# Two more block products of the first layer's MLP up-projection by seven products in place of eight

## What is computed

```python
h2 = rmsnorm(x, g_mlp)                                   # 256 x 1024
x = x + jnp.square(jax.nn.relu(h2 @ w_up)) @ w_down      # w_up 1024 x 4096, w_down 4096 x 1024
```

## Time and profile before

| | us |
|---|---|
| median of 3 runs | 979.6 |
| lowest and highest | 979.2, 980.6 |
| the profiled execution | 979.45 |
| its span in the trace | 977.6 |
| TensorE busy in the span | 969.5 |
| VectorE busy | 759.6 |
| ScalarE busy | 518.2 |

### The profile page before, as it was taken

How to read it: one execution, slowest core, us unless ns; L and a number is a source line. 1 busy time by engine, 2 the same in 40 slices (tenths; PEclk the granted TensorE clock), 3 DMA queues, 4 the chain that set the end, 5 groups by cost and what they waited for, 6 DMA issues and landing times.

```text
span 977.6 us, 12897 instructions
## 1 busy us (share of the span) xinstructions
PE 969.5 (99%) x5174; PEld 811.5 (83%) x5174; DVE 759.6 (78%) x848; ACT 518.2 (53%) x619; POOL 129.2 (13%) x101
## 2 busy tenths in 40 slices
PE   9999999999999999999999999999999999999997
PEld 7888888888888888888888888888887899799696
DVE  5878886766978766778886776988777788789984
ACT  6656553465566445556563464543487454644352
POOL 0000000000000000000000010000000159269820
PEclk9999999999999999999999999999999999999999
DMA  9887796669972994697796669899774957346351
GB/s 361 305 281 277 237 270 211 232 222 321 344 234 86 268 270 129 186 302 250 249 272 209 225 226 245 260 281 287 239 248 140 295 179 259 131 164 160 107 194 44
DMA packets 142684, 224.78 MB, mean 230 GB/s; under 512 B 11808, under 2 KB 50720, under 8 KB 142368
## 3 DMA queue, kind: packets, MB, share of 16 engines
q1 hardware_dynamic: 142624, 223.95, 72.0%
HBM read 199.32 MB, written 22.28 MB: 227 GB/s over the span
## 4 chain that ended last, share of the span: by engine, by line
PE 98%; DMA 1%; DVE 0%; ACT 0%; issue 0%; POOL 0%; DVEq 0%; SPq 0%; ACTq 0%
PE bank L1061 15%; PE bank L1064 15%; PE bank L1063 15%; PE bank L1084 13%; PE bank L1088 12%; PE bank L1095 12%; PE bank L1507 2%; PE bank L1808 1%; PE bank L1616 1%; PE bank L1579 1%; PE bank L1199 1%; PE bank L1176 1%; PE bank L1289 1%; PE bank L1795 1%; PE bank L1093 1%; PE bank L1086 1%
## 5 line engine op out<-in xcount | busy, mean ns | idle before, releaser
L2348 DVE TENSOR_TENSOR w_lo<-arena,w_hi 128x2048 fp32r<-128x2048 f32 (+1 forms) x84 | 192.6, 2301 | 52.3 <-ACT w_hi L1903 51.9
L2348 DVE TENSOR_TENSOR w_lo<-raw,w_hi 128x2048 fp32r<-128x2048 f32 (+1 forms) x76 | 173.6, 2290 | 56.9 <-ACT w_hi L1903 56.7
L1903 ACT ACTIVATE w_hi<-arena 128x2048 fp32r<-128x2048 f32 (+1 forms) x84 | 158.7, 1891 | 82.1 <-PE bank L1064 71.5
L1903 ACT ACTIVATE w_hi<-raw 128x2048 fp32r<-128x2048 f32 (+1 forms) x81 | 153.1, 1891 | 73.8 <-PE bank L1064 61.2
L1061 PE MATMUL bank<-w_hi,hT 128*128 128x512 f32 (+1 forms) x336 | 129.5, 385 | 0.0
L1064 PE MATMUL bank<-w_hi,hT 128*128 128x512 f32 (+1 forms) x320 | 122.8, 384 | 0.0
L1063 PE MATMUL bank<-w_lo,hT 128*128 128x512 f32 (+1 forms) x320 | 122.8, 384 | 0.0
L1084 PE MATMUL bank<-w_hi,hT 128*128 128x512 f32 (+1 forms) x316 | 121.5, 386 | 0.0
L1088 PE MATMUL bank<-w_hi,hT 128*128 128x512 f32 (+1 forms) x316 | 120.9, 384 | 0.0
L3230 POOL TENSOR_TENSOR rstd<-mean,const 128x1 f32<-128x1 f32 (+1 forms) x16 | 9.1, 576 | 615.9 <-DVE mean L2357 456.7
L1095 PE MATMUL bank<-w_lo,hT 128*128 128x512 f32 (+1 forms) x316 | 82.8, 384 | 0.0
(11 more groups left out here) (375 smaller groups left out, 1799.1 us busy)
## 6 DMA issues: line engine op xcount, KB each, us to landing
arena<-in_w_in SPq DMA_DIRECT2D x21, 1024.0 KB, 6.4
raw<-in_w_in SPq DMA_DIRECT2D x20, 1024.0 KB, 6.8
arena<-in_w_down SPq DMA_DIRECT2D x20, 1024.0 KB, 6.4
raw<-in_w_up SPq DMA_DIRECT2D x18, 1024.0 KB, 7.5
arena<-in_w_up SPq DMA_DIRECT2D x14, 1024.0 KB, 7.8
raw<-in_w_down SPq DMA_DIRECT2D x12, 1024.0 KB, 7.2
arena<-u_bounce SPq DMA_DIRECT2D x72, 128.0 KB, 4.7
u_bounce<-arena SPq DMA_DIRECT2D x17, 512.0 KB, 6.3
```

The lines of the kernel that those rows point to most:

```text
L1903: act.activation(w_hi[:, p % SPLIT_RING, :, 0:n], raw_at(p)[:, :, 0:n], copy).then_inc(hi_ready, 1)
L2348: dve.tensor_tensor(w_lo[:, s, :, 0:n], raw_at(p)[:, :, 0:n], w_hi[:, s, :, 0:n].bitcast(F32), ALU.subtract).then_inc(lo_ready, 1)
```

## The change

`PAIRED` becomes `(4, 6)`: groups 4 and 5 are a pair too. The steps are up 0, 1, 2, down 0, up 3, first 4, down 1, rest 4, down 2, down 3, first 6, rest 6, down 4 to 7. So the first pair's five products stand right behind up 3, and the seven products of the second pair stand in a row. The sums of the token operands are made once and serve both pairs; the weight differences are made for each pair. The four raw pieces of the second pair go into slots that the first pair has used up (six slots for both pairs, `PAIR_B11` and so on). The product that went to bank 7 in `pair_rest` goes to bank 6. For the second pair ScalarE waits, before it copies the first product, until the store of group 5 has landed (`rows_stored`), and TensorE waits for the banks of both groups of the first pair. In SP's order the four loads of groups 4 and 5 stand earlier, and those of groups 6 and 7 behind waits for the sums "first 0" and "second 0" and for splits of the first pair.

```diff
-PAIRED_STEPS = [("up", 0), ("up", 1), ("up", 2), ("down", 0), ("up", 3), ("down", 1), ("up", 4), ("up", 5), ("first", 6),
-                ("down", 2), ("rest", 6)] + [("down", f) for f in range(3, F_GROUPS)]
-SUMS_AFTER = {1: ("rows 2",), 3: ("rows 0",), 4: ("rows 1", "third"), 5: ("rows 3",), 6: ("first", "second"), 9: ("fourth",)}
+PAIRED_STEPS = [("up", 0), ("up", 1), ("up", 2), ("down", 0), ("up", 3), ("first", 4), ("down", 1), ("rest", 4), ("down", 2),
+                ("down", 3), ("first", 6), ("rest", 6)] + [("down", f) for f in range(4, F_GROUPS)]
+SUMS_AFTER = {1: ("rows 2", "rows 0"), 2: ("rows 1",), 3: ("rows 3", "third 0"), 4: ("first 0", "second 0"), 6: ("fourth 0",),
+              8: ("third 1",), 9: ("first 1", "second 1"), 10: ("fourth 1",)}
...
-PAIRED = (6,)
+PAIRED = (4, 6)
...
-PAIR_B11, PAIR_B12, PAIR_B22, PAIR_B21, PAIR_T3, PAIR_T2 = ((i,) for i in range(6))
+PAIR_B11, PAIR_B12, PAIR_B22, PAIR_B21 = (0, 1), (1, 0), (2, 4), (3, 2)
+PAIR_T3, PAIR_T2 = (4, 5), (5, 3)
...
-TURNED_IN = [{2: 0, 3: 1, 5: 2, 7: 3, 11: 4, 12: 5, 13: 6, 14: 7}, INNER_TURNS]
+TURNED_IN = [{2: 0, 3: 1, 6: 2, 8: 3, 10: 4, 12: 5, 13: 6, 14: 7}, INNER_TURNS]
...
                 up(2, 0)
+                load_pair(0, PAIR_B12, 1, 1)
                 up(2, 1)
+                load_pair(0, PAIR_B22, 1, 0)
                 down(0, 0)
                 down(0, 1)
                 store_up(l, 0)
+                load_pair(0, PAIR_B11, 0, 1)
                 up(3, 0)
                 fetch_up(l, 0)
-                load_pair(0, PAIR_B12, 1, 1)
                 up(3, 1)
+                load_pair(0, PAIR_B21, 0, 0)
                 store_up(l, 1)
...
                 for t in range(T):
-                    pe.wait_ge(out_free[t], n - 1)
+                    pe.wait_ge(out_free[t], n if i else n - 1)
...
-                pe.wait_ge(pair_sum, 3 * i + 2)
-                pair_product(p, 7, *pair_sums(3), False).then_inc(piece_used, 1)
+                pe.wait_ge(pair_sum, 3 * i + 1)
+                pair_product(p, 6, *pair_sums(3), True).then_inc(piece_used, 1)
...
                         act.wait_ge(piece_used, q + 1)
+                        if f != PAIRED[0]:
+                            act.wait_ge(rows_stored, 16 * (2 * T + f + 1))
                         act.activation(pair_p1, bank[:, 0, :], copy).then_inc(pair_taken, 1)
...
                     if kind == "first":
                         step(q + 2)
+                        if i == 10:
+                            operand_sum("fourth 1")
                         step(q + 3)
                         pair_base(PAIRED.index(f))
                         step(q + 4)
```

More of the change, by code:

```diff
@@ L106 @@
         PAIR_PIECES[at] = PAIR_SLOT + slots[i]
-PAIR_SUMS = {FIRST_OF[0] + 1: "third", FIRST_OF[0] + 4: "first", FIRST_OF[0] + 3: "second", REST_OF[0] + 1: "fourth"}
+PAIR_SUMS = {}
+for i in range(len(PAIRED)):
+    PAIR_SUMS.update({FIRST_OF[i] + 1: f"third {i}", FIRST_OF[i] + 4: f"first {i}", FIRST_OF[i] + 3: f"second {i}",
+                      REST_OF[i] + 1: f"fourth {i}"})
 ANGLES_AT = 2
@@ L2627, in operand_sum @@
                 elif name == "rows 1":
-                    for i, a in enumerate(hidden(1, 0)):
-                        order.link(dve.tensor_tensor(full[1], full[i], a, ALU.subtract))
+                    for src, a in enumerate(hidden(1, 0)):
+                        order.link(dve.tensor_tensor(full[1], full[src], a, ALU.subtract))
                     parts(1)
@@ L2635, in operand_sum @@
                     parts(3)
-                elif name == "third":
-                    dve.wait_ge(middle_landed, 16 + 32)
+                elif kind == "third":
+                    dve.wait_ge(middle_landed, 16 + 32 * (i + 1))
                     weights(PAIR_T3, PAIR_B22, PAIR_B12)
-                elif name == "first":
-                    dve.wait_ge(pair_outer, 32)
+                elif kind == "first":
+                    dve.wait_ge(pair_outer, 32 * (i + 1))
                     weights(PAIR_B12, PAIR_B12, PAIR_B11)
-                elif name == "second":
+                elif kind == "second":
                     weights(PAIR_T2, PAIR_B22, PAIR_B12)
                 else:
-                    piece_split(dve, FIRST_OF[0] + 2)
+                    piece_split(dve, FIRST_OF[i] + 2)
                     weights(PAIR_B21, PAIR_B21, PAIR_T2)
@@ L2680, in pair_second @@
                 order.settle()
-                order.link(dve.tensor_tensor(by_block(pair_c), by_column(bank[:, 7, :]), by_column(pair_w), ALU.add))
+                order.link(dve.tensor_tensor(by_block(pair_c), by_column(bank[:, 6, :]), by_column(pair_wp), ALU.add))
                 square_rows(pair_wp, pair_c).then_inc(out_free[0], 2)
@@ L2897, in _ @@
                         for name in SUMS_AFTER.get(i, ()):
-                            if name != "fourth":
+                            if not name.startswith("fourth"):
                                 operand_sum(name)
```

37 lines of the change are left out of this document (21 added, 16 removed).

## The result

| | before | after |
|---|---|---|
| median | 979.4 us (4 runs) | 998.3 us (4 runs, 997.5 to 999.8) |
| profiled execution | 979.45 | 999.78 |
| its span | 977.6 | 997.9 |
| TensorE busy | 969.5 | 973.8 |
| VectorE busy | 759.6 | 780.0 |

The changed kernel is slower: ratio 1.0193, with an interval of 1.0175 to 1.021. That is 18.9 us by the medians and 20.3 us from one profiled execution to the other. The forecast was 992.9, the range 985.0 to 999.0.

The account below looks back on a forecast made before the run. The prediction took TensorE to bound the kernel, with no slack, so each wait costs one for one. It summed -2.7 + 4.2 + 1.0 + 7.0 + 3.8 = +13.3 us to 992.9 us, range 985.0 to 999.0.

Parts of the forecast that it names:

- the second rival with its lower bounds: Rival: only VectorE delays, the queue's loads go through in idle time; 986.9 us, chance 0.22; lower bounds set the range's 985.0.
- Place 1: First two fetches: 3 MB more loads ahead of each delay down 0 and the first pair; +4.2 us.
- Place 2: Last product of rest 4: a transposition and uT_lo ahead of `pair_fourth` use up the conversion's slack; +1.0 us.
- Place 3: Second pair, seven products in a row: the seventh waits for VectorE's list of splits, differences and steps; +7.0 us.
- Place 4: Down 6: its rows, from the seventh product, come late after VectorE's steps, store and fetch; +3.8 us.
- 28.7 against 21.8: Second pair, us from the first down 3 piece's end: VectorE's list against TensorE reaching the seventh product; 6.9 late.
- 2 us of it I give back: Before down 6: store and fetch taken 2 us under the earlier 16.7, group 5's fetch no longer being queued.
- R + 9.7: Before down 6: VectorE's steps take 9.7 us from R, the start of the second pair's seventh product.
- R + 24.5: TensorE wants down 6 24.5 us after R, the seventh product's start: that product plus down 4 and 5.
- Nothing gives it back: Whole sum of +13.3 us: TensorE runs on at the same pace behind each wait.
- the clock falls as well: Rival: TensorE's clock halves behind three waits, some 1.5 us each, +4.5 in all; 997.4 us, chance 0.13.
- All is hidden: Rival: no waits, only the 2.7 us saved; 976.9 us, needing VectorE's second-pair list 7 us shorter; chance 0.05.

Follow-up runs that it names:

- the kernel with six waits: Kernel before the change, with six waits put in front of down 1 to down 6 of the second layer's MLP: 1014.8 us (one execution).
- The kernel with the new order: Changed kernel with both SP queue edits and VectorE's pair steps and some differences placed earlier, no work taken from VectorE: 979.1 us, ratio 0.9999.
- short differences and the new order: New-order kernel with three more VectorE moves, and the second pair's four weight differences formed over 16 of 512 columns: 977.0 us, ratio 0.9978.
- the kernel kept busy: Changed kernel with unread matmuls on TensorE in its waits: 12 before rest 6, 11 within it, 24 before down 6: 996.0 us, ratio 1.0165.
- short differences: Changed kernel with the second pair's three weight differences formed over 16 of 512 columns only: 996.3 us, ratio 1.017.
- the loads for down 6 first: Changed kernel with the two loads for down 6 ahead of the stores of groups 6 and 7 in SP's queue: 991.1 us, ratio 1.0108.

## Why the prediction was right, and where it was not

The direction was right, and so was the reason for it: each of the four places lost time. The size was short, +13.3 for +18.9, and 998.3 lies only 0.7 us inside the range; the profiled execution is outside it. The upper end of 999.0 had room for bigger terms or for the clock, not for both, and that it still held the result is in part luck. (Its lower end, "the second rival with its lower bounds", sums to 984.4 and not 985.0.)

| term | forecast | measured in the profiled execution |
|---|---|---|
| 12 matmuls saved | -2.7 | -2.7 |
| 1. first two fetches | +4.2 | 3.3, with small pauses 3.5 |
| 2. last product of rest 4 | +1.0 | 1.5, with the pauses behind it 2.0 |
| 3. second pair in a row | +7.0 | 0.9 + 3.1 + 2.9 = 6.9, with small pauses 7.1 |
| 4. down 6 | +3.8 | 6.1 |
| lower clock | 0 (rival: +4.5) | +4.4 |
| sum | +13.3 | +20.4 (20.3 between the executions) |

- **What bounds the kernel**: right. Every wait put in front of TensorE was lost one for one; the kernel with six waits shows the same where nothing else changes.
- **Place 1**: the mechanism is shown by its undoing (3.5 us back), and the size was 0.7 too high. The second transposition was 3.8 late, not 4.7.
- **Place 2**: the mechanism agrees with the view of waits, TensorE waits for `w_hi` of the difference "fourth" there; no run priced it alone. Mis-sized by 1.0. The prediction sets 2.4 us of new work against 2.3 of slack, which gives about 0; it took 1.0. In the changed kernel VectorE also came to `pair_base` 1.3 us later beside TensorE (274.89, where down 1 begins at 273.50; before, 302.35 and 302.28), and behind the conversion TensorE had pauses of 0.5 in sum for its split.
- **Place 3**: the sum (28.7 against 21.8) met the wait within 0.1, and the three waits came where they were said to come. But the reading that a shorter list would shorten the wait was wrong by half: with 6.7 us of differences taken away only 3 us of waits went. Beside the list stands the order: two splits between `pair_base` and `pair_fourth`, the second of which needs the slot of the fifth product. The kernel with the new order has the same work for VectorE (busy 779.9 us, 780.0 in the changed kernel) and none of these three waits; one of 1.0 for a split is left there. And cured at this place alone, the time comes back at down 6.
- **Place 4**: the step that failed is "2 us of it I give back". Store and fetch took 16.2 us (348.6 to 364.8), as long as the 16.7 of the earlier trace rows, since 2 MB for down 6 are issued between the store and the fetch in both kernels. Before, the wait for them was hidden. Without that rebate the prediction's own sum is 6.5, not 4.5, and it then took 3.8 for it; 6.1 was measured. Two more differences nearly cancel: VectorE's part was 1.8 longer (R + 11.5 for R + 9.7; the rows give 10.3 for the steps that it names, and 1.2 are idle time for a conversion that waits for the seventh product), and TensorE came 1.7 later than R + 24.5, for the clock.
- **"Nothing gives it back: behind each wait TensorE runs on at the same pace"**: wrong. The forecast gave 0.13 to the case that the clock falls as well, and priced it at 4.5 us; it came true at 4.4, beside all four terms. That the sizes agree is in part luck: it named three falls of 1.5 us, and there were two, of 9 and 13 matmuls. The sentence of the Trainium skill (TensorE: Matmul & The Clock Gate, "Why this matters for your kernels") was the only witness, because the kernel before never waited over 1.0 us. The trace now agrees that idle gaps in mid-kernel bring the half rate back, though not behind each gap. It stood as a rival where it should have stood in the sum.
- **All is hidden**, the rival for faster, needed VectorE's list to be shorter; the kernel with short differences and the new order is that case, at 977.0 where it said 976.9. The shorter list was named rightly as a condition, but is not enough (996.3 with it alone). That order alone gives back all but 2.2 us (979.1) was not foreseen.

## What to carry to other kernels

When a forecast puts waits of some us in front of TensorE, price the clock too. Each stretch at the lower level cost 1.4 to 3.0 us here (7 matmuls of 128x512 at 0.2 more in the shortest, 15 in the longest, behind the 2.9 us of the kernel with `pair_fourth` put forward), a fifth of the whole loss in the changed kernel. A wait removed at one place of a full engine's list comes back at the next, so read that engine's list to its end before placing a step, and look in the queue for loads that could have gone before a store that waits. Seven products for eight cost VectorE 20.4 us for 2.7 of TensorE: worth it only where VectorE has that much free in the very stretch, not in the mean.

## What was not expected of the hardware

- **The length of a wait alone does not tell whether the clock falls.** A wait of TensorE of 1.8 us (behind one of 2.2, 31 us earlier, in the kernel kept busy) was followed by nine matmuls at 1.2 GHz. One of 2.7 (short differences), one of 2.3 (the loads for down 6 first) and two of 2.2 us (kept busy, GpSimd) were followed by none. All of 2.9 us and longer were, though in the changed kernel, and in that with the loads for down 6 first, only behind the next wait, of 2.7.
- **The fall can begin inside the wait**, so that a longer wait does not cost more clock: behind 8.0 us only 8 matmuls ran at the lower level, behind 5.75 us 10, behind 2.6 us 8 (the six waits), and behind the 6.0 before down 6 in the changed kernel 13.
- **GpSimd beside VectorE**: a 128x2048 subtraction took GpSimd 5.5 us in the mean (4.7 to 6.5) and VectorE 2.3, and VectorE's instructions stood still meanwhile. Work moved to an idle GpSimd was slower than the same work left on a nearly full VectorE, by 22 us of the whole.
